# Two passes of 256 columns in place of one of 512 in every dense product of a two-block transformer kernel

## The chip, the cores and the metric

The kernel runs on one core of a Trainium2 chip. The metric is the device time of one execution in microseconds. TensorE multiplies a stationary operand of up to 128 x 128 values, which a weight load brings in, with a moving operand that streams through it column by column, and adds the products up in a PSUM bank of 128 x 512 fp32 values.

## The reference, cut to what matters

Two transformer blocks run one after the other on 512 tokens of width 1024. The first has two layers, each with two attentions (one over indexed keys, one latent), a gated merge, an output projection and an FFN with a convolution over the tokens. The second has one layer, with dilated, compressed, selected and windowed attention and a SiLU FFN. The change touches only products with weight matrices, of which these stand for all:

```python
z = h @ w_in[l]
x = x + merged @ w_out[l]
u = causal_dwconv(h @ w_up[l], conv_w[l], conv_b[l])
x = x + (jax.nn.silu(gat) * val) @ w_down[l]
```

## The kernel before, in words

Activations are kept transposed, features on the 128 partitions and the 512 tokens along the free dimension. So a product with a weight matrix is made of tiles of 128 output features by 512 tokens, a full PSUM bank each, into which the products with the 128 x 128 blocks of one column of the weight matrix are added.

To reach fp32 accuracy with the fast fp32r form, each operand is held as an upper and a lower part. The helper `matmul` (L509) makes one block product of three passes: lower weights by upper activations, upper by lower, upper by upper. Each pass is one call of `pe.matmul`, which becomes a weight load of the stationary operand and a matmul. `linear`, `linear_pair`, `linear_tiles` and `token_major` are loops over block products; in `token_major` the activations are stationary and the weights move.

Weights are streamed. SyncE brings tiles of eight blocks into `weight_ring` (four slots), GpSimd splits each tile into `w_hi` (L1948) and `w_lo` (L1954), two slots each, and TensorE waits on `weights_split` at the first block of each tile. The first pass that uses a tile signals `weights_begun`, and GpSimd then may overwrite the slot of the tile before it. The last pass of an output tile signals `tile_done`; VectorE or ScalarE then empties the bank and signals `taken`, and the bank is used again four tiles later.

Each engine runs its own list of instructions in the order in which the code is written. The two layers of the first block are a hardware loop on TensorE (L704), and so is the main part of each half of an FFN: L879 in the first block (two halves a layer, so it runs four times) and L1042 in the second (twice). Each of these six runs makes five rounds of four tiles; a round has 4 x 8 block products, 96 passes.

Some passes are not 512 columns wide: the index queries (`tokens=slice(P, S)`, 384), the second block's values (width 280), the hidden layer of the compressor (`hidden`, 256, made of operands in the arena alone) and three small products of 64.

Of the kernel before, what the change touches and what calls it, by code (L numbers as in the profile page):

```python
# [23 lines left out]
S = 512  # L24
# [65 lines left out]
                 out=64, up=352, down=176)  # L90
# [178 lines left out]
def two_blocks_kernel(nc, x_t, stream, w1, w2, par1, par2, consts, rows32, rows8, tables, spread, out_t, rows, scratch):  # L269
    with ExitStack() as ctx:  # L270
# [3 lines left out]
        def sem(name):  # L274
            return ctx.enter_context(nc.semaphore(name))
# [25 lines left out]
        def chunks(first, n):  # L301
            return arena[:, first:first + n, :]
# [39 lines left out]
        ksl, kw, v2 = chunks(47, 2), chunks(49, 2), chunks(51, 2)  # L342
# [24 lines left out]
        weights_begun = sem("weights_begun")  # L367
# [78 lines left out]
        def prob(n, width):  # L446

            n %= PROBS
            return work[:, n, 0:width] if n < 6 else sq[:, n - 6, 0:width]

        def block_bank(n):

            return (turn + stat)[n]
# [52 lines left out]
        def _(pe):  # L506
            state = {"block": 0, "begin": False}

            def matmul(out, lhs, rhs, start, stop, **kw):  # L509


                for n, (l, r) in enumerate(((lhs[1], rhs[0]), (lhs[0], rhs[1]), (lhs[0], rhs[0]))):
                    ins = pe.matmul(out, l, r, start=start and n == 0, stop=stop and n == 2, **kw)  # L513
                    if state["begin"]:
                        ins.then_inc(weights_begun, 1)
                        state["begin"] = False
                return ins

            def stage(sec, L, tiles, base):
# [179 lines left out]
            for bank, to, rows_n, table, at, width in bias_parts:  # L699
                pe.matmul(bank[0:rows_n, to:to + width], tab[:, table:table + rows_n], onehot[:, at:at + width],  # L700
                          start=True, stop=True).then_inc(rows_done, 1)


            with pe.Fori(0, LAYERS) as L:  # L704
# [20 lines left out]
                for n, key in enumerate(BESIDE_INDEX):  # L725
# [5 lines left out]
                    for q in index_batch(n):  # L731
                        b, h = INDEX[q]
                        r = slice(h % 2 * HD, h % 2 * HD + HD)
# [8 lines left out]
                for key, lhs in ((("krr",), ident), (("krp",), perm)):  # L742
                    ps = bank(key)
                    plain(pe)
                    for i in range(4):
                        ins = pe.matmul(ps[32 * i:32 * i + 32, :], lhs[32:64, 32:64], misc[32:64, 0, :], start=True,
                                        stop=True)
# [123 lines left out]
                for part, (first, n) in enumerate(HALVES):  # L871
                    n0 = A.tile_no(("up", 2 * first))
                    v0, at = A.release[n0][1], state["block"]
# [5 lines left out]
                    with pe.Fori(1 - part, n // 2) as i:  # L879
                        for s in (0, 2):  # L880

                            for k in range(DC):
                                for e in range(2):
                                    if k == 0:
                                        pe.wait_ge(A.taken["v"], L * A.count["v"] + i * 4 + (v0 + s + e - 4))
                                    w = weight(i, 4)
                                    ins = matmul(psum[(n0 + s + e) % 4][:, :], w, h_ffn(k), start=(k == 0),
                                                 stop=(k == DC - 1))
# [75 lines left out]
            def turn_compared(b):  # L964
                def turns():
                    pe.wait_ge(cmp_masked, QB)
                    pe.wait_ge(cmp_prob, b + 1)
                    plain(pe)
                    for g in range(2):
                        ins = pe.transpose(block_bank(b)[:, g * P:(g + 1) * P], work[:, b, g * P:(g + 1) * P], ident)  # L970
                    ins.then_inc(cmp_turn, 1)
                return turns
# [61 lines left out]
            for part, (first, n) in enumerate(HALVES):  # L1034
                n0 = B.tile_no(("gate", first))
                v0, a0, at = B.release[n0 + 1][1] - 1, B.release[n0][1] - 1, state["block"]
# [5 lines left out]
                with pe.Fori(1 - part, n // 2) as i:  # L1042
                    for s in (0, 2):
# [3 lines left out]
                        for k in range(DC):  # L1047
                            for e in range(2):
                                if (k, e) == (0, 1):
                                    pe.wait_ge(B.taken["v"], i * 2 + (v0 + s // 2 - 1))  # L1050
                                w = weight(i, 4)
                                ins = matmul(psum[(n0 + s + e) % 4][:, :], w, h_ffn(k), start=(k == 0),
                                             stop=(k == DC - 1))
# [8 lines left out]
        def _(act):  # L1062
# [243 lines left out]
            def block_uppers(first):  # L1306

                for n in range(first, first + 2):
                    act.wait_ge(blocks_raw, n + 1)
                    act.activation(blocks_hi[:, :, 32 * n:32 * n + 32],  # L1310
                                   block_bank(n)[:, :].rearrange("p (k n) -> p k n", n=32), ACT.Copy).then_inc(blocks_upper, 1)
# [952 lines left out]
```

## Time and profile before

| | |
|---|---|
| median of three runs | 2345.83 us (2345.34 to 2346.99) |
| the profiled execution | 2345.93 us |
| its span, first to last instruction | 2344.1 us |
| TensorE matmul busy | 2309.0 us, 11106 matmuls |
| TensorE weight load busy | 1759.3 us, 11106 loads |
| GpSimd busy | 1571.7 us |
| VectorE busy | 1073.8 us |
| ScalarE busy | 618.5 us |
| moved by DMA | 212.65 MB |

Matmuls overlap: one is shown from its start to the end of its results, while the next has already begun. The pace is therefore read from the distance between starts, not from the mean length. Weight loads (PEld) run beside the matmuls. Engine names in the rows are PE and PEld for the two sides of TensorE, DVE for VectorE, ACT for ScalarE, POOL for GpSimd and SP for SyncE.

### The profile page before, as it was taken

The page shows a single profiled execution, that of the slowest core. Times are in us where ns is not written, and L with a number is a line of the kernel's source. Part 1 is how long each engine was busy: PE and PEld are TensorE (multiplying, and loading weights), DVE is VectorE, ACT ScalarE, POOL GpSimd, SP SyncE. Part 2 cuts the span into 40 slices and gives each one's busy share as a digit, 9 for nine tenths or more (in the row PEclk, how much of TensorE's full clock was granted, in tenths as well). Part 3 has the DMA queues.
Part 4 walks back from the last instruction along what each step waited for, and adds up shares of the span by engine and source line. Part 5 has one row for each costly group of instructions (what it writes and reads, how often), then busy time and mean ns, then how long its engine had stood idle before and what let it go on. Part 6 is the DMA issues. An engine that isn't in the chain of part 4 may idle for free. (4 is left out here: it accounts for less than half of the span.)

```text
span 2344.1 us, 34637 instructions
## 1 busy us (share of the span) xinstructions
PE 2309.0 (99%) x11106; PEld 1759.3 (75%) x11106; DVE 1073.8 (46%) x2156; ACT 618.5 (26%) x1355; POOL 1571.7 (67%) x818
## 2 busy tenths in 40 slices
PE   7999999999999999999999999999999999999997
PEld 5666688878888876666888788888787667888886
DVE  5776643364314346776534643143545854110112
ACT  4334710231001233347202311012322863000001
POOL 6564377777777775643677777777766437777775
PEclk9999999999999999999999999999999999999999
DMA  6223023223233232220232232323372002323322
GB/s 208 72 78 103 11 81 99 90 90 96 92 95 94 91 99 65 80 99 20 73 98 92 89 98 90 98 90 96 131 225 90 29 19 90 91 98 91 98 90 90
DMA packets 61586, 212.65 MB, mean 91 GB/s; under 512 B 6344, under 2 KB 6728, under 8 KB 61328
## 3 DMA queue, kind: packets, MB, share of 16 engines
q1 hardware_dynamic: 54368, 194.38, 26.6%
q10 hardware_dynamic: 7088, 16.58, 2.1%
q8 instruction: 76, 1.25, 0.2%
q14 instruction: 54, 0.44, 0.1%
HBM read 208.78 MB, written 10.01 MB: 93 GB/s over the span
## 5 line engine op out<-in xcount | busy, mean ns | idle before, releaser
L513 PE MATMUL out_tile<-arena_r,w_hi 128*128 128x512 f32 (+1 forms) x5240 | 1641.1, 394 | 0.0
L513 PEld LDWEIGHTS out_tile<-arena_r,w_hi 128*128 128x128 f32 x5240 | 984.7, 188 | 232.1 <-issue 1.9
L513 PE MATMUL out_tile<-arena_r,w_lo 128*128 128x512 f32 (+1 forms) x2620 | 1042.2, 398 | 9.3 <-POOL w_lo L1954 6.5
L1948 POOL TENSOR_TENSOR w_hi<-weight_ring,cst 128x1024 fp32r<-128x1024 f32 (+1 forms) x348 | 656.3, 1886 | 536.0 <-PE out_tile L513 473.1
L1954 POOL TENSOR_TENSOR w_lo<-weight_ring,w_hi 128x1024 fp32r<-128x1024 f32 (+1 forms) x348 | 835.7, 2402 | 26.9
L513 PEld LDWEIGHTS out_tile<-arena_r,w_lo 128*128 128x128 f32 x2620 | 492.8, 188 | 152.4 <-issue 26.4
L1469 DVE TENSOR_TENSOR x<-out_tile,x 128x512 f32<-128x512 f32 x72 | 49.8, 691 | 360.4 <-PE out_tile L513 360.3
L1287 ACT ACTIVATE work<-out_tile,p 128x512 f32<-128x512 f32 x88 | 65.8, 773 | 412.1 <-PE out_tile L513 412.1
L1734 DVE SCALAR_TENSOR_TENSOR work<-out_tile,p,work 128x511 f32<-128x511 f32 x88 | 65.6, 745 | 224.6 <-ACT work L1287 224.6
L1973 POOL TENSOR_SCALAR work<-work,small 128x128 f32<-128x128 f32 (+2 forms) x60 | 34.8, 580 | 114.0 <-DVE small L1522 106.7
L1152 ACT ACTIVATE arena<-turned 128x128 f32<-128x128 f32 (+1 forms) x224 | 84.8, 430 | 47.2 <-PE turned L662 46.3
L1159 ACT ACTIVATE work<-work,small 128x128 f32<-128x128 f32 (+1 forms) x168 | 83.7, 503 | 49.8 <-DVE small L1514 49.8
L513 PE MATMUL out_tile<-w_hi,arena_r 128*128 128x512 f32 (+1 forms) x288 | 88.7, 379 | 0.0
L1381 ACT ACTIVATE work<-out_tile 128x512 f32<-128x512 f32 x22 | 13.2, 598 | 281.4 <-PE out_tile L513 281.4
L679 PE MATMUL stat<-arena 128*64 128x128 f32 x1120 | 85.7, 283 | 0.0
L1085 ACT ACTIVATE arena_r<-x,p 128x512 fp32r<-128x512 f32 x48 | 34.6, 720 | 184.0 <-DVE x L1469 184.0
L1514 DVE CUSTOM_DVE_ANT_0 work<-out_tile,arena 128x128 f32<-128x128 f32 (+1 forms) x168 | 64.7, 419 | 30.5 <-PE out_tile L837 13.7
L1269 ACT ACTIVATE work<-out_tile,p 128x512 f32<-128x512 f32 x32 | 22.0, 689 | 210.7 <-PE out_tile L513 210.7
L679 PEld LDWEIGHTS stat<-arena 128*64 128x64 f32 x1120 | 58.8, 136 | 21.4 <-issue 20.8
L513 PEld LDWEIGHTS out_tile<-w_hi,arena_r 128*128 128x128 f32 x288 | 52.3, 188 | 16.7 <-issue 6.9
L1705 DVE TENSOR_TENSOR work<-out_tile,work 128x512 f32<-128x512 f32 x14 | 9.7, 693 | 110.2 <-PE out_tile L513 110.2
L662 PEld LDWEIGHTS turned<-cst,work 128*128 128x128 f32 x336 | 36.2, 140 | 27.5 <-issue 13.8
(223 smaller groups left out, 1912.8 us busy)
## 6 DMA issues: line engine op xcount, KB each, us to landing
weight_ring<-stream SPq DMA_DIRECT2D x356, 512.0 KB, 3.5
arena<-bias_rows ACTq DMA_DIRECT2D x4, 2048.0 KB, 11.7
bias_rows<-bias_kept ACTq DMA_DIRECT2D x2, 2556.0 KB, 24.2
bias_rows<-bias_kept SPq DMA_DIRECT2D x1, 2556.0 KB, 14.9
x<-x_t SPq DMA_DIRECT2D x4, 512.0 KB, 8.7
arena<-w ACTq DMA_DIRECT2D x1, 2048.0 KB, 8.8
out_t<-arena SPq DMA_DIRECT2D x8, 256.0 KB, 2.2
cst<-consts SPq DMA_DIRECT2D x1, 576.0 KB, 14.0
```

The costliest lines, as they stand in the source:

```text
L513: ins = pe.matmul(out, l, r, start=start and n == 0, stop=stop and n == 2, **kw)
L662: ins = pe.transpose(turn[n % 2][0:width, k * P:(k + 1) * P], prob(n, k * P + width)[:, k * P:k * P + width], ident)
L679: ins = pe.matmul(stat[group % 2][e * HD:(e + 1) * HD, b * P:(b + 1) * P], values(pair[e], k), turned[0:width, 2 * (m % SLOTS) + e, k * P: ...
L1152: act.activation(turned[:, m % (2 * SLOTS), 0:w], turn[m % 2][:, 0:w], ACT.Copy)\
L1159: act.activation(prob(n, w), prob(n, w), ACT.Exp, scale=-1.0, bias=negmax[:, n % 8:n % 8 + 1], accum_out=rsum[:, n % 8:n % 8 + 1])\
L1287: act.activation(work[:, s, :], psum[(n0 + s) % 4][:, :], ACT.Identity, scale=p1[:, bass.ds(c + 2, 1)], bias=p1[:, bass.ds(c + 3, 1)])\
L1469: took(dve.tensor_tensor(x[:, j, :], tile(sec, L, key(j))[:, :], x[:, j, :], ALU.add), sec)
L1514: took(dve.tensor_tensor_reduce(prob(n, w), ps[:, 0:w], masks, 1.0, 3e38, ALU.add, ALU.min, negmax[:, c:c + 1]), sec)
L1734: dve.scalar_tensor_tensor(out=work[:, s, 1:S], in0=ps[:, 0:S - 1], scalar=p1[:, bass.ds(c + 1, 1)], in1=work[:, s, 1:S], op0=ALU.mult, op ...
L1948: pool.tensor_tensor(blocks_of(w_hi[:, s % SPLIT, :], used), blocks_of(ring[:, s, :], used), cols(cst, C_ONE).unsqueeze(1).to_broadcast([P ...
L1954: pool.tensor_tensor(blocks_of(w_lo[:, s % SPLIT, :], used), blocks_of(ring[:, s, :], used), blocks_of(w_hi[:, s % SPLIT, :].bitcast(F32), ...
L1973: pool.tensor_scalar(part, part, rinv[:, n % 8:n % 8 + 1], 1.0 if gate is None else gate, ALU.mult, ALU.mult).then_inc(sec.prob_even, 1)
```

## The change

Where the output of a block product is 512 columns wide, each of its three passes is issued as two, over the tokens (or output columns) 0 to 255 and 256 to 511, into the two halves of the same bank. Each half has its own weight load of the same stationary operand. The start flag is set on the first half of the first pass alone, and the first half signals `weights_begun`; the stop flag of the last pass is on both halves, and `tile_done` is signalled by the second.

```diff
--- before.py
+++ after.py
@@ -448,6 +448,8 @@
             n %= PROBS
             return work[:, n, 0:width] if n < 6 else sq[:, n - 6, 0:width]
 
+        token_halves = (slice(0, S // 2), slice(S // 2, S))
+
         def block_bank(n):
 
             return (turn + stat)[n]
@@ -509,11 +511,15 @@
             def matmul(out, lhs, rhs, start, stop, **kw):
 
 
+                halves = token_halves if out.shape[-1] == S else (slice(0, out.shape[-1]),)
+                if len(halves) > 1:
+                    kw["skip_group_check"] = True
                 for n, (l, r) in enumerate(((lhs[1], rhs[0]), (lhs[0], rhs[1]), (lhs[0], rhs[0]))):
-                    ins = pe.matmul(out, l, r, start=start and n == 0, stop=stop and n == 2, **kw)
-                    if state["begin"]:
-                        ins.then_inc(weights_begun, 1)
-                        state["begin"] = False
+                    for h, at in enumerate(halves):
+                        ins = pe.matmul(out[:, at], l, r[:, at], start=start and n == 0 and h == 0, stop=stop and n == 2, **kw)
+                        if state["begin"]:
+                            ins.then_inc(weights_begun, 1)
+                            state["begin"] = False
                 return ins
 
             def stage(sec, L, tiles, base):
```

TensorE's list at the head of the FFN loop L879, before the change. A row names the output and, behind the arrow, the two operands; x2 means two equal ones in a row; the register row belongs to the wait for a free bank (L885):

```order
L513 MATMUL out_tile<-arena_r,w_lo 128x512
L513 MATMUL out_tile<-arena_r,w_hi 128x512 x2
L885 REGISTER_ALU
L513 MATMUL out_tile<-arena_r,w_lo 128x512
L513 MATMUL out_tile<-arena_r,w_hi 128x512 x2
L513 MATMUL out_tile<-arena_r,w_lo 128x512
L513 MATMUL out_tile<-arena_r,w_hi 128x512 x2
```

And the same place after the change, where six more lines stand ahead in the file:

```order
L519 MATMUL out_tile<-arena_r,w_lo 128x256 x2
L519 MATMUL out_tile<-arena_r,w_hi 128x256 x4
L891 REGISTER_ALU
L519 MATMUL out_tile<-arena_r,w_lo 128x256 x2
L519 MATMUL out_tile<-arena_r,w_hi 128x256 x4
L519 MATMUL out_tile<-arena_r,w_lo 128x256 x2
L519 MATMUL out_tile<-arena_r,w_hi 128x256 x4
```

Each row of passes has become twice as many of half the width; the rows stand in the same order and nothing has moved past anything else.

## Rows read from the trace of the kernel before

**Rows 1.** The page: busy time, and the span in 40 slices.
```profile
PE 2309.0 (99%) x11106; PEld 1759.3 (75%) x11106; DVE 1073.8 (46%) x2156; ACT 618.5 (26%) x1355; POOL 1571.7 (67%) x818
...
PEclk9999999999999999999999999999999999999999
```

**Rows 2.** Groups of TensorE matmuls by form: count | busy us, mean ns.
```profile
L513 PE MATMUL out_tile<-arena_r,w_hi 128*128 128x512 f32 x5112 | 1607.5, 395 | 0.0
L513 PE MATMUL out_tile<-arena_r,w_lo 128*128 128x512 f32 x2556 | 1018.7, 399 | 4.8 <-POOL w_lo L1954 2.0 <-DVE arena_r L1496 1.1 <-DVE work L1742 1.0
L513 PE MATMUL out_tile<-w_hi,arena_r 128*128 128x512 f32 x224 | 75.9, 403 | 0.0
L513 PE MATMUL out_tile<-w_lo,arena_r 128*128 128x512 f32 x112 | 43.9, 392 | 0.0
```

**Rows 3.** Waits of TensorE: us in total, times, longest us.
```profile
PE stat L700 <- DMA cst<-consts: 10.0, 1, 10.0
PE out_tile L513 <- POOL w_lo L1954: 6.5, 8, 2.0
```

**Rows 4.** Timeline of GpSimd in an FFN stretch: start us, us.
```profile
601.27 1.89 POOL L1948 TENSOR_TENSOR w_hi<-weight_ring,cst 128x1024 fp32r<-128x1024 f32 x1 [1.23 <-PE out_tile L513]
...
606.87 1.89 POOL L1948 TENSOR_TENSOR w_hi<-weight_ring,cst 128x1024 fp32r<-128x1024 f32 x1 [1.24 <-PE out_tile L513]
```

**Rows 5.** Timeline of TensorE in the last FFN.
```profile
2240.36 0.40 PE L513 MATMUL out_tile<-arena_r,w_lo 128*128 128x512 f32 x1
...
2242.46 0.39 PE L513 MATMUL out_tile<-arena_r,w_lo 128*128 128x512 f32 x1
```

**Rows 6.** Timeline, passes of 280 columns.
```profile
1717.61 0.29 PE L513 MATMUL out_tile<-w_lo,arena_r 128*128 128x280 f32 x1
...
1719.90 0.29 PE L513 MATMUL out_tile<-w_lo,arena_r 128*128 128x280 f32 x1
```

**Rows 7.** Groups of TensorE weight loads.
```profile
L513 PEld LDWEIGHTS out_tile<-arena_r,w_hi 128*128 128x128 f32 x5240 | 984.7, 188 | 232.1 <-issue 1.9
```

**Rows 8.** Timeline and line view (ns min/median/max) of the 256-column passes.
```profile
1720.53 2.31 PE L513 MATMUL stat<-arena_r 128*128 128x256 f32 x18
1728.29 3.74 PE L513 MATMUL stat<-arena_r 128*128 128x256 f32 x30
1728.87 2.23 PEld L513 LDWEIGHTS stat<-arena_r 128*128 128x128 f32 x18
L513 PEld LDWEIGHTS stat<-arena_r x48: 187/192/192, 1720.4 to 1731.6; 128*128 128x128 f32 x48
L513 PE MATMUL stat<-arena_r x48: 274/283/283, 1720.5 to 1731.7; 128*128 128x256 f32 x48
```

**Rows 9.** Windows: us, busy PE, PEld, DVE, ACT, POOL, clock, DMA share, GB/s.
```profile
1818.00:1828.00 10.00, 10.00 (x98) 6.57 (x96) 8.57 (x33) 8.55 (x28) 5.38 (x5) 1.00 0.11 27
1728.40:1731.70 3.30, 3.30 (x30) 3.30 (x29) 0.69 (x1) 0.00 (x0) 0.00 (x0) 1.00 1.01 329
2200.00:2260.00 60.00, 60.00 (x259) 48.35 (x258) 10.41 (x15) 2.99 (x5) 45.53 (x23) 1.00 0.30 96
935.00:950.00 15.00, 15.00 (x66) 8.58 (x65) 11.53 (x19) 6.30 (x12) 6.68 (x4) 0.89 0.23 72
```

**Rows 10.** The page: instruction queue of TensorE; packets, MB.
```profile
q8 instruction: 76, 1.25, 0.2%
```

**Rows 11.** DMA in the windows 480 to 512, 512 to 600, 838.5 to 838.65.
```profile
q8 instruction: 2, 0.03, 0.4%
...
q1 hardware_dynamic: 2293, 8.34, 30.9%
...
q8 instruction: 1, 0.02, 58.0%
```

**Rows 12.** Timeline of TensorE over the layer loop's jump.
```profile
841.02 0.63 PE L513 MATMUL out_tile<-arena_r,w_hi 128*128 128x512 f32 x2
841.66 0.44 PE L513 MATMUL out_tile<-arena_r,w_lo 128*128 128x384 f32 x1
```

## The prediction

> **What bounds the kernel now.** I read the page first. TensorE is busy for 2309.0 of 2344.1 us, 99%, and the granted clock is at its upper level, 2.4 GHz, nearly throughout [rows 1]. A busy matmul engine need not be at its peak, since the bars of neighbouring matmuls overlap: a dense pass of 512 columns is shown as 392 to 403 ns long [rows 2], but starts well before the last one has ended. So the second view is the list of its waits: 10.0 us for the constants at the start, then 6.5 us in eight waits for split weights, and all others are shorter [rows 3]. There is nothing under which a slower TensorE could hide: what a pass takes longer, the kernel takes longer. GpSimd, which prepares the weights, starts a tile each 5.60 us and idles 1.23 or 1.24 us of them for TensorE [rows 4]; it has slack.
>
> The third view is the timeline, for the true pace. In a dense stretch the w_lo pass of one block product starts at 2240.36 and that of the third after it at 2242.46 [rows 5]: nine passes in 2.10 us, 0.2333 us a pass, or 0.456 ns a column. Passes of 280 columns take 2.29 us for six block products, 18 passes (1717.61 to 1719.90) [rows 6], 0.1272 us, 0.454 ns a column. So down to 280 columns the time is proportional to the columns, with no part per pass, and the weight load of each pass is fully hidden behind the pass before.
>
> **The change part by part.** It touches the dense passes whose output is 512 columns wide: 5112 + 2556 + 224 + 112 into the output tiles [rows 2], and 24 (eight block products) of the keys that `last_keys` computes, 8028. The 192 of 384 columns, 96 of 280, 48 of 256 and 9 of 64 keep their form, and so do the fp32 products of the attention.
>
> *Columns:* none are added or taken away; 2 x 256 is 512.
>
> *Weight loads:* 8028 more, of 128 columns. One load shows as 0.188 us [rows 7], which is longer than a pass of 256 columns would be at the proportional pace (0.456 x 256 = 0.1167 us), so it must overlap its own neighbours to stay hidden. Whether it does, the trace shows at one place: the compressor's 48 passes of 256 columns, each with its own 128 x 128 load, the form that the change makes of everything. There 18 loads from the inside of the run of 30 take 2.23 us from the first start to the last end; less the 0.192 us of one, 17 spacings are 2.038 us, 0.1199 us each. The two whole runs of matmuls give (2.31 - 0.283)/17 and (3.74 - 0.283)/29, both 0.1192 us [rows 8]. In the window of that stretch the load engine is busy for all of 3.30 us, where it is busy for 48.35 of 60 in a dense stretch of 512 columns [rows 9]. So at 256 columns the load is no longer free: some 3 ns of each pass stick out. For the pace of the changed kernel I take 0.1199 us, that of the inside of a run, since nearly all its passes stand in long runs. Two of them are 0.2398 us in place of 0.2333: 6.5 ns more. Times 8028 that is **+52 us**. With 0.1192, which holds the quick first passes of a run, it is 5.1 ns and +41 us. The lower bound is zero, at the proportional 0.1167; a gain is excluded because no row, at 280 or 512 columns, holds a cost per pass that a shorter pass could shed. The upper bound, for want of a nearer row, is the pace of the 280-column passes, 0.1272: 21 ns more, +169 us; the 256-column row is the same operation, so I stay near it.
>
> The Trainium skill (TensorE: Matmul & The Clock Gate, "Wait — 56ns, not 53.3ns?") gives a warm matmul N/2.4 GHz and about 2.5 ns fixed, which hides the load entirely. By that two halves would cost one more fixed part, 2.5 ns, and the change +20 us. The rows differ from it at both widths (0.2333 and 0.1199 us against 215.8 and 109.2 ns), and the sum follows the rows.
>
> *Instructions:* TensorE has twice as many dense ones to take in. It must sustain a load and a matmul in each 0.1199 us. In the attention it starts 98 matmuls in 10.00 us [rows 9], 0.102 us each, with semaphore waits among them, so the supply is fast enough. Nothing is charged.
>
> *Instruction fetches:* 76 transfers of the instruction queue feed TensorE [rows 10]; they will be some 60 more of 16 KB, nothing beside 212 MB. What can cost is a jump. At the layer loop's jump back, a fetch runs at 838.5 to 838.65 us [rows 11]; TensorE goes on from what it had taken in until the pass at about 841.26 (the second of the row at 841.02), and the next starts at 841.66: 0.40 instead of 0.233 us, 0.17 us lost [rows 12]. From about 838.6 it lived on some 11.4 queued passes; the weight load there comes 3.05 us after the fetch. With half the columns 11.4 passes last 1.4 us, so 1.6 us stick out. This jump is taken once: **+1.4 us**.
>
> *Waits:* the first half signals weights_begun, and with the same columns per product the tile's time grows from 5.6 to 5.76 us, which gives GpSimd more slack; part of the 6.5 us of waits for it shrinks. **-1 us**; bounds 0 and -6.5.
>
> *Semaphores, banks, order:* the last pass of a tile carries tile_done as before; the same four banks are used in the same order. Nothing.
>
> **Sum:** 52 + 1.4 - 1 = +52 us. The profiled execution took 2345.93 us, 1.8 more than its span and 0.1 from the median, 2345.83, so the sum goes onto the median: **2398 us**, +2.2%.
>
> **The rivals.**
> *The halves run at the proportional pace, no change.* The extra 3 ns could belong to the one stretch in which they were seen: there both operands lie in the arena, one accumulator region is hit by every pass, and the DMA engines are full (share 1.01, 329 GB/s [rows 9]). In the dense stages the weights lie in w_hi and w_lo, the halves alternate, and the share is 0.30. Against it: the 280-column passes ran beside the same traffic at the proportional pace, and all of a 256-column run shows the load engine full. It decides if the load's own pace is below 0.1167 us. Then 2 x 0.1167 is 0.2333: 2346 us. Chance 0.12, which holds the small chance of a hair faster. If only some of the passes run at 0.1167, the time lies between, 2355 to 2380: 0.09. The fixed part of the page named above, +20 us, would be 2366 and fall into this case.
>
> *The FFN loops no longer stay resident.* The six inner FFN loops take their jump back four times each, 24 in all. Today none fetches: from 512 to 600 us the weights' queue is the only one with packets, while 480 to 512 has two fetches [rows 11]. One fetch holds about (22212 - 24 x 192)/76 = 232 of the matmuls and loads [rows 1, 10]; a loop's body is 96 passes and 96 loads, 0.8 of a fetch, and becomes 384, 1.7 fetches, so that it can lie over three blocks. If the engine keeps too few, each jump fetches as the layer's does: 24 x 1.6 = 38 us more, 2436 us; uncovered, 24 x 3.05 = 73, 2471 us. For it: the layer's jump shows what a miss is. Against: the present loops are held with a block border inside almost surely and no fetch at all. Chance 0.12. The Trainium skill (Runtime: NRT & Kernel Launch, "Instruction fetch mechanics") says both that TensorE holds 128 KiB in 16 KiB blocks, by which the bigger body fits, and that the window is two blocks, by which it would not; no row here decides between them.
>
> *The clock falls.* Between 935 and 950 us the granted clock averages 0.89 [rows 9], although the engine was busy throughout. If fewer columns per microsecond made this common, each such dip would cost under 2 us; it takes ten to matter. Chance 0.03, 2420 us.
>
> **How the numbers follow.** Main case 0.64 (2384 to 2408, from +41 us less waits to +6.5 ns a pass with a rough fetch); no change 0.12; between 0.09; loops 0.12; clock 0.03. The range 2362 to 2440 leaves out the no-change case, a part of the mix and the upper half of the loop case, some 0.2. A change of 0.2% (4.7 us) is about what a measurement here tells from none: faster by more 0.02, within it 0.09, slower 0.89.
>
> **What would show it.** In the profile after: 256-column passes by the thousand, whose starts in a dense stretch lie 0.120 us apart, twelve in 1.44 us; the load engine near 100% busy in the FFN, with loads of about 0.192 us; GpSimd's idle time per tile near 1.4 us; waits of TensorE no longer than now; granted clock at 1.00; no instruction fetch inside the loops. Right on the time but wrong on the step would be a pace of 0.1167 with gaps of 1.6 us at each jump. Wrong altogether: a pace under 0.118 or over 0.122, or idle time of TensorE put down to issue.

## The result, and the profile after

The change made the kernel a little faster, and the times wider apart. The median went from 2346.54 us (22 runs, 2345.29 to 2349.98) to 2332.38 us (22 runs, 2317.03 to 2354.22). The ratio is 0.9939, 95% interval 0.9924 to 0.9954: 0.6% faster, where 2.2% slower was forecast. The ratio leaves out the slowest of the 22, which lies more than 1.5% above the fastest, though its granted clock (0.996) is that of the others. The changed kernel spreads over 37 us, that of before over 5.

The page of the profiled execution of the changed kernel (its span is 2331.8 us, its own time 2333.62 us); these are its lines on busy time, the granted clock and the queue of instruction fetches:

```profile
PE 2293.4 (98%) x19134; PEld 2119.8 (91%) x19134; DVE 1068.9 (46%) x2156; ACT 618.7 (27%) x1355; POOL 1573.6 (67%) x818
PEclk9999999999999999999999999999999999999999
q8 instruction: 121, 1.98, 0.4%
```

The dense passes in the list of groups with each shape apart:

```profile
L519 PE MATMUL out_tile<-arena_r,w_hi 128*128 128x256 f32 x10224 | 1598.6, 279 | 0.0
L519 PE MATMUL out_tile<-arena_r,w_lo 128*128 128x256 f32 x5112 | 1016.9, 280 | 4.9 <-POOL w_lo L1960 2.6 <-DVE work L1748 1.0 <-DVE arena_r L1502 0.5
```

The longest waits of TensorE behind that for the constants (line, what it waited for, us in total, times, longest):

```profile
PE out_tile L519 <- POOL w_lo L1960: 7.5, 9, 2.0
PE out_tile L519 <- DVE arena_r L1466: 2.5, 1, 2.5
```

TensorE does twice the number of dense instructions and is still the bound, as in [rows 1]; no long wait is new beside [rows 3] but one of 2.5 us, at the layer loop's jump. The load engine is shown as 91% busy. So the difference lies in the pace, and the timeline shows it. The fence holds TensorE in two stages and at the layer loop's jump, and GpSimd between:

```profile
379.86 0.40 PE L519 MATMUL out_tile<-arena_r,w_lo 128*128 128x256 f32 x2
...
380.57 0.40 PE L519 MATMUL out_tile<-arena_r,w_lo 128*128 128x256 f32 x2
...
559.96 0.39 PE L519 MATMUL out_tile<-arena_r,w_lo 128*128 128x256 f32 x2
...
560.64 0.39 PE L519 MATMUL out_tile<-arena_r,w_lo 128*128 128x256 f32 x2
...
574.01 1.90 POOL L1954 TENSOR_TENSOR w_hi<-weight_ring,cst 128x1024 fp32r<-128x1024 f32 x1 [1.07 <-PE out_tile L519]
579.46 1.89 POOL L1954 TENSOR_TENSOR w_hi<-weight_ring,cst 128x1024 fp32r<-128x1024 f32 x1 [1.06 <-PE out_tile L519]
...
834.22 0.62 PE L519 MATMUL out_tile<-arena_r,w_hi 128*128 128x256 f32 x4
837.33 0.44 PE L519 MATMUL out_tile<-arena_r,w_lo 128*128 128x384 f32 x1 [2.49 <-DVE arena_r L1466]
```

A block product (three passes of 512 columns before, six of 256 now) takes 0.71 us at 380 and 0.68 us at 560 us; before it took 0.700 everywhere [rows 5]. So there are two paces, one below and one above the old one. The windows give them better, with the passes of 100 us in the brackets behind PE's busy time (columns: window, its length, PE, its weight loads, DVE, ACT, POOL, granted clock, DMA share, GB/s):

```profile
340.00:440.00 100.00, 100.00 (x851) 100.00 (x851) 39.81 (x32) 8.67 (x14) 77.56 (x36) 1.00 0.30 95
550.00:650.00 100.00, 100.00 (x885) 100.00 (x884) 34.17 (x54) 12.14 (x18) 78.45 (x37) 1.00 0.30 95
1150.00:1250.00 100.00, 100.00 (x851) 100.00 (x850) 37.10 (x30) 8.18 (x12) 78.43 (x36) 1.00 0.30 96
1450.00:1550.00 100.00, 100.00 (x884) 100.00 (x884) 27.52 (x43) 9.54 (x14) 79.19 (x37) 1.00 0.30 95
2050.00:2150.00 100.00, 100.00 (x851) 100.00 (x851) 11.79 (x17) 1.79 (x3) 75.61 (x36) 1.00 0.30 94
```

885 passes in 100 us are 0.1130 us each, 851 are 0.1175. A window also counts the passes that cross its two borders; by the starts of block products in the timeline the two are 0.1133 us (0.680 us a product) and 0.1178 us (0.7067 us). I call them the quick and the slow rhythm. Clock, DMA share and traffic are the same in both. Every window has one or the other, held for hundreds of passes, and nothing between.

### The profile page after: what moved, and what is told of

It reads as the page before. It is cut to its first block and busy times, and to the rows that moved or that the text cites. A ratio compares the mean times of both kernels' runs of the same rounds, so it can differ in the third digit from the quotient of the medians.

```text
span 2331.8 us, 50693 instructions
## 1 busy us (share of the span) xinstructions
PE 2293.4 (98%) x19134; PEld 2119.8 (91%) x19134; DVE 1068.9 (46%) x2156; ACT 618.7 (27%) x1355; POOL 1573.6 (67%) x818
## 5 line engine op out<-in xcount | busy, mean ns | idle before, releaser
L519 PE MATMUL out_tile<-arena_r,w_hi 128*128 128x256 f32 (+1 forms) x10352 | 1632.8, 280 | 0.0
L519 PEld LDWEIGHTS out_tile<-arena_r,w_hi 128*128 128x128 f32 x10352 | 1391.6, 189 | 0.5 <-issue 0.5
L519 PE MATMUL out_tile<-arena_r,w_lo 128*128 128x256 f32 (+1 forms) x5176 | 1040.9, 282 | 12.2 <-POOL w_lo L1960 7.5
L519 PEld LDWEIGHTS out_tile<-arena_r,w_lo 128*128 128x128 f32 x5176 | 790.9, 189 | 40.7 <-issue 29.1
L519 PE MATMUL out_tile<-w_hi,arena_r 128*128 128x256 f32 (+1 forms) x512 | 89.6, 286 | 0.0
L519 PEld LDWEIGHTS out_tile<-w_hi,arena_r 128*128 128x128 f32 x512 | 72.2, 188 | 8.0 <-issue 6.9
```

Of the source, the lines that this page charges most:

```text
L519: ins = pe.matmul(out[:, at], l, r[:, at], start=start and n == 0 and h == 0, stop=stop and n == 2, **kw)
```

## The experiments

Each kernel is the changed one with the edit shown. Without an interval a time is that of one execution.

**The changed kernel again, twice.** Does the place in the program set the rhythm, or the execution?

> The changed kernel, not altered, run again. Its first profile shows two paces of the 256-column passes: 0.1133 us (layer FFNs and output products, 532 passes in 60 us) and 0.1178 us (gates and projections, last FFN, 512 passes in 60 us). Theory of the place: the pace belongs to the stage, by its operands and the traffic beside it; then every stage shows its pace again, within 2 passes per 60 us, and the span is within 3 us of 2331.8. Theory of the lock: a run of passes falls into one of two paces by how it begins and keeps it; then at least one long stage shows the other pace in this or the next run, and the span moves with it by 4.4 ns for each pass of that stage (about 13 us for the last FFN).

> The same kernel once more, unaltered. Theory of the place: the same paces in the same stages, span within 3 us of 2331.8. Theory of the lock: stages differ from the first profile or from the run before this one; the spans spread by more than 5 us.

Measured: 2339.12 and 2331.93 us. The same five windows, of the first:

```profile
340.00:440.00 100.00, 100.00 (x851) 100.00 (x850) 39.98 (x32) 8.82 (x14) 77.59 (x36) 1.00 0.30 96
550.00:650.00 100.00, 100.00 (x852) 100.00 (x851) 34.61 (x55) 12.15 (x18) 75.87 (x36) 1.00 0.28 90
1150.00:1250.00 100.00, 100.00 (x885) 100.00 (x884) 38.75 (x30) 8.83 (x13) 82.17 (x38) 1.00 0.31 101
...
2050.00:2150.00 100.00, 100.00 (x885) 100.00 (x884) 14.56 (x21) 2.99 (x5) 78.24 (x38) 1.00 0.29 96
```

and of the second:

```profile
340.00:440.00 100.00, 100.00 (x885) 100.00 (x884) 41.32 (x34) 12.38 (x19) 82.21 (x38) 1.00 0.30 98
550.00:650.00 100.00, 100.00 (x852) 100.00 (x851) 30.86 (x48) 10.71 (x16) 75.56 (x37) 1.00 0.29 95
```

The window at 340 is slow in the first two executions and quick in the third; the one at 550 is quick in the first and slow in the other two. One program, the same stages, another rhythm: it is set in each execution anew, and then holds.

By steps of 0.0200 us down or 0.0067 up for each of 2676 block products (8028 / 3), all quick is 54 us less and all slow 18 us more; the 22 runs lie within these two ends.

These rhythms account for the spread. In the timelines, 8222 passes of the first profile of the changed kernel begin a row of six at the quick pace and 7027 a row of six at the slow one; in the second profile 6723 and 8555, in the third 8119 and 7130. Priced by a sixth of these steps for each pass, the second should be 6.7 us longer than the first and the third 0.5 us longer; their spans are 5.5 us longer and 1.7 us shorter (the third lacks a fall of the clock that cost the first 1.6 us; see the part on the clock). Two kernels with the same passes that follow below, one in another order and one with added waits, have 11198 and 4028, and 5245 and 9980: priced 13 us shorter and 13 longer than the first profile, measured 11.9 shorter and 12.9 longer.

**A small disturbance.** An fp32 transpose into a spare bank ahead of each pair of output tiles in the last FFN's loops.

```
+                        pe.transpose(turn[1][:, 0:P], ident, ident)
```

> The changed kernel with one fp32 transpose of 128 columns, of constants into a bank that is idle then, ahead of each pair of output tiles in the loops of the last FFN (20 of them). It costs some 0.2 us each time, 4 us in all. Theory of the lock: each transpose ends a run of passes, so the pace of the last FFN is drawn anew each 11 us: stretches of 0.1133 appear in it, between stretches of 0.1178, or all of it goes to one of them. Theory of the place: the last FFN stays at 0.1178 throughout and the span is 4 us longer, 2336.

Measured: 2323.96 us. The last FFN now holds both rhythms, changing from one pair of tiles to the next: 1982 to 1991 us has 82 passes, 1993 to 2002 has 79, where the three executions of the changed kernel each kept one rhythm through it. Of the 20 pairs, each opened by its transpose, 7 go by the quick rhythm and 13 by the slow one; each keeps its own to the end, and from one pair to the next it changes eight times. So a foreign matmul can throw the row over, either way. The total says little here, since the stages before the last FFN drew their rhythms anew as well.

**The load's own pace.** The layers' FFN as 384 + 128 and 320 + 192 columns, the last FFN as 4 x 128 and uncut.

```
+                    state["widths"] = ((384, 128), (320, 192))[part]
+                state["widths"] = ((128, 128, 128, 128), (512,))[part]
```

> The changed kernel with other cuts of the 512 columns by stage: 384 + 128 in the first half of the FFNs of the layers, 320 + 192 in their second half, 4 x 128 in the first half of the last FFN, 512 uncut in its second half. If a load and a pass go side by side and the longer sets the pace, with the load at about 0.112 us (the nine passes of 64 columns), then a 128-column pass takes 0.112, a block product of three passes 3 x (0.175 + 0.112) = 0.86 us in the first stage, 3 x (0.146 + 0.112) = 0.77 in the second and 12 x 0.112 = 1.34 in the third, and the uncut stage 0.70; span about 2331.8 + 98 + 40 + 188 = 2660 us. If the load costs nothing of its own and only columns count, all stages take 0.68 to 0.70 us a block product and the span stays within 15 us of 2331.8.

Measured: 2652.33 us. One window for each pattern, in that order:

```profile
600.00:660.00 60.00, 60.00 (x421) 60.00 (x420) 18.64 (x29) 6.71 (x10) 36.61 (x18) 1.00 0.25 79
800.00:860.00 60.00, 60.00 (x467) 60.00 (x466) 22.39 (x35) 11.19 (x18) 42.54 (x20) 1.00 0.28 87
2100.00:2160.00 60.00, 60.00 (x540) 60.00 (x539) 13.64 (x20) 4.07 (x7) 23.33 (x12) 1.00 0.16 51
2500.00:2560.00 60.00, 60.00 (x259) 48.46 (x258) 11.81 (x17) 3.59 (x6) 45.75 (x22) 1.00 0.31 94
```

Passes of 128 columns take 60/540 = 0.111 us (0.1117 from the timeline) although their columns are half of 256. The times are those expected of a load that sets the pace (0.86, 0.77 and 1.34 us a block product). In the timeline the loads of this stage begin 50 to 55 ns behind the start of the pass before, where they begin 1 to 5 ns behind it with 256 or 512 columns throughout: here one load is held back by another, and there it is not. So 0.1117 us is the pace at which loads of 128 columns follow each other. It lies under the proportional 0.1167, so a load need not make a 256-column pass longer. The uneven pairs take 0.287 (0.1433 x 2) and 0.258 us, the uncut pass 0.2333: short passes below the load's pace are dear.

**Nearly even cuts.** 264 + 248 and 272 + 240 in the layers' FFN, 288 + 224 and 256 + 256 in the last.

```
+                    state["widths"] = ((264, 248), (272, 240))[part]
+                state["widths"] = ((288, 224), (256, 256))[part]
```

> The changed kernel with uneven halves by stage: 264 + 248 in the first half of the FFNs of the layers, 272 + 240 in their second, 288 + 224 in the first half of the last FFN, 256 + 256 in its second. Theory of the load: at 0.113 us a pass is set by the back-to-back loads (0.112 us), so a part under 256 columns gains nothing and one over it costs its columns: by the proportional pace 0.120 + 0.112 = 0.232 (first), 0.124 + 0.112 = 0.236 (second), 0.131 + 0.112 = 0.243 us (third) for two parts, against 0.227 or 0.236 at 256 + 256; only the even cut can be under 0.2333. Theory of the columns: the stall that a short pass sheds depends on its own width, and two parts of uneven width share it: all cuts down to 240 take 0.227 to 0.236 and show two paces each.

Measured: 2359.2 us; pairs of 0.2371, 0.2378 and 0.2467 us, and 0.2267 (the quick rhythm) for the even cut. Only the even cut is under 0.2333, as the first of the two theories said. Neither set of numbers was met, and I have no rule for these three; of the cuts tried, the even one alone gains, so it is not short passes as such.

**Another order.** All three passes of the first half, then those of the second.

```
+                for h, at in enumerate(halves):
+                    for n, (l, r) in enumerate(passes):
```

> The changed kernel with the order of the six passes of a block product turned: the three of the first half, then the three of the second, so that only the two upper passes load the same block in a row. If the lower pace needs the same block to be loaded twice in a row, or the two halves of one row to follow each other, every stage goes to another pace (117.8 ns or more throughout, span at least 2350). If it belongs to the width alone and to how the run begins, long stages again show 0.1133 or 0.1178 us and nothing else, and the span lies within 2305 to 2355.

Measured: 2321.67 us, with the same two rhythms (885, 884, 885, 885 and 852 passes in the five windows). Of six neighbouring pairs of passes, four load the same block twice in the changed kernel and two in this one; the halves of one pass no longer follow each other. So neither of the two is needed for the rhythms. Whether they need any such pair at all was not tried.

**One pass of three cut.** Only the w_lo pass of each block product is cut; the other two stay at 512.

```
-                    for h, at in enumerate(halves):
+                    for h, at in enumerate(halves if n == 0 else (slice(0, out.shape[-1]),)):
```

> One part of the change alone: the first of the three passes of a block product (lower weights) is cut into halves, the two others stay at 512 columns. 2676 cut passes in place of 8028. If each cut pass sheds its own share of the gain, a block product takes 0.4667 + 0.227 = 0.693 us at the quick pace or 0.4667 + 0.2356 = 0.702 at the slow one, and the span lies between 2344 - 18 and 2344 + 7. If the gain needs an unbroken row of short passes, since it is the loads one behind the other that set the pace, all stages take 0.700 us a block product, as before, and the span is within 3 us of 2344.

> The kernel with only the first pass of each block product cut, timed against the kernel before. If its one pace of 0.6933 us a block product belongs to the form, all its executions lie within 3 us of 2331, a ratio of 0.9935 (0.993 to 0.994). If it too has a second pace that one profile missed, its executions spread over more than 10 us, as those of the changed kernel did (2317 to 2354).

Measured: 2331.09 us, and in the timed comparison 2330.58 us (5 runs, 2330.08 to 2332.68), ratio 0.9936, interval 0.9923 to 0.995. The timeline:

```profile
599.75 0.39 PE L519 MATMUL out_tile<-arena_r,w_lo 128*128 128x256 f32 x2
599.98 0.62 PE L519 MATMUL out_tile<-arena_r,w_hi 128*128 128x512 f32 x2
600.44 0.40 PE L519 MATMUL out_tile<-arena_r,w_lo 128*128 128x256 f32 x2
```

A block product takes 0.693 us in every stage, and the spread is 2.6 us, not 37. The same gain as by cutting everything, with a third of the extra instructions, and steady. A long row of short passes is not needed for it.

**TensorE waits for its own last tile** at the start of five stages, so that each begins with an empty pipe.

```
+                        A.wait_done(pe, L, ("up", 3))
+                        plain(pe)
```

> The changed kernel with TensorE made to wait for its own last tile at five places, ahead of the gates of each layer, of the FFN loop of each layer and of the last FFN's loop, so that it stops for some 0.3 us and the long run begins after a true stop. In the three profiles 12 of 13 runs that began after a gap of about 0.52 us, a stop, went to 0.1133 us. If the start of a run decides and a stop leads to the quick pace, all five long stages (1548, 2970, 1548, 2970 and 3000 passes) show 885 passes in 100 us, and the span is that of the first profile less 4.45 ns x (1554 + 1554 + 3018) = 27 us, plus 2 for the stops: 2307. If a stop leads to no pace in particular, some of the five show 851, and the span stays in 2315 to 2355.

Measured: 2346.54 us; four of the five windows are slow (851, 885, 851, 852, 851). A stop does not lead to the quick rhythm. This theory fell.

**Which pass is cut.** By stage: the third alone; the first two; the last two; the first and third; the second alone.

```
+                state["cut"] = (2,)
+                    state["cut"] = ((0, 1), (1, 2))[part]
+                state["cut"] = ((0, 2), (1,))[part]
```

> Which passes of a block product are cut, by stage: gates and projections the third alone, first half of the layers' FFNs the first two, their second half the last two, first half of the last FFN the first and third, its second half the second alone, all else the first alone. Measured so far: no cut 0.700 us a block product, the first alone 0.6933 in every stage, all three 0.680 or 0.7067. Theory of the share: each cut pass among uncut ones sheds 6.7 ns, so one cut gives 0.6933 (578 passes in 100 us) whichever it is, two give 0.6867 (728 passes in 100 us), and every stage has one pace; the span is about 2344 - 6.7 ns x (2676 + 1152 + 864) = 2313. Theory of the row: what brings the two paces is a long row of cut passes without an uncut one; with any uncut pass in the product the pace is one and steady, but two cuts need not give twice one. Theory of the weights: only the pass with the lower weights sheds, as its load comes from the other tile; then gates and projections and the second half of the last FFN stay at 0.700 (571 passes in 100 us).

Measured: 2350.21 us. Windows with the third alone, the first two, the last two, and the first and third:

```profile
340.00:440.00 100.00, 100.00 (x579) 87.70 (x578) 40.93 (x33) 10.23 (x16) 79.93 (x37) 1.00 0.30 95
550.00:650.00 100.00, 100.00 (x710) 93.41 (x708) 33.22 (x52) 12.16 (x18) 75.67 (x36) 1.00 0.30 95
1450.00:1550.00 100.00, 100.00 (x709) 93.40 (x708) 20.61 (x33) 7.47 (x11) 75.50 (x36) 1.00 0.30 95
2050.00:2150.00 100.00, 100.00 (x709) 93.41 (x708) 13.88 (x20) 3.00 (x5) 76.96 (x36) 1.00 0.29 94
```

One cut is 0.6933 us a product whichever pass it is (four passes, 579 in 100 us; the second alone, at 2220 to 2250 us, has the same by its starts); two cuts are 0.7067 whichever two (five passes, 709): more cuts, and slower than none. No theory that adds up a price per cut pass can hold. What counts is the pattern of short and long.

**Patterns.** By stage, over successive block products: one cut and none in turn; seven with all cut and then one with none; all and one; all and none; one and two.

```
+                pattern = state.get("cut", ((0,),))
+                cut = pattern[state.get("product", 0) % len(pattern)]
```

> Patterns over block products, by stage (all: three passes cut; one: the first cut; two: the first two; none). Gates and projections: one, none in turn. First half of the layers' FFNs: seven times all, then none. Second half: all, one in turn. First half of the last FFN: all, none in turn. Second half: one, two in turn. All else: one. Measured so far per block product: none 0.7000, one 0.6933, two 0.7067, all 0.6800 or 0.7067 us. If the pace is a sum over products, the means are 0.6967, then 0.6825 or 0.7058, then 0.6867 or 0.7000, then 0.6900 or 0.7033, then 0.7000 us. If it is a matter of the repeating pattern as a whole, as two cuts costing more than one or none suggest, the means are others, each still a whole number of steps of 6.67 ns over its period; and a single uncut product in eight makes the layers' first FFN half one pace in both layers.

Measured: 2334.67 us; means of 0.700, 0.6937, 0.6867, 0.695 and 0.6967 us a product. A sum of the paces of the single products would have been 0.6967, 0.6825 or 0.7058, 0.6867 or 0.7000, 0.6900 or 0.7033, and 0.7000: it holds for the third alone. The second pattern shows what happens at each uncut product:

```profile
600.65 0.64 PE L522 MATMUL out_tile<-arena_r,w_hi 128*128 128x256 f32 x4
601.12 0.39 PE L522 MATMUL out_tile<-arena_r,w_lo 128*128 128x512 f32 x1
601.35 0.63 PE L522 MATMUL out_tile<-arena_r,w_hi 128*128 128x512 f32 x2
601.82 0.39 PE L522 MATMUL out_tile<-arena_r,w_lo 128*128 128x256 f32 x2
602.05 0.62 PE L522 MATMUL out_tile<-arena_r,w_hi 128*128 128x256 f32 x4
602.50 0.39 PE L522 MATMUL out_tile<-arena_r,w_lo 128*128 128x256 f32 x2
...
606.58 0.39 PE L522 MATMUL out_tile<-arena_r,w_lo 128*128 128x512 f32 x1
606.81 0.63 PE L522 MATMUL out_tile<-arena_r,w_hi 128*128 128x512 f32 x2
...
607.51 0.64 PE L522 MATMUL out_tile<-arena_r,w_hi 128*128 128x256 f32 x4
607.98 0.40 PE L522 MATMUL out_tile<-arena_r,w_lo 128*128 128x256 f32 x2
```

Ahead of 601.12 four passes of w_hi take 0.47 us; behind the three long ones they take 0.45 (602.05 to 602.50); at 606.58 three long ones come again, and it is 0.47 again (607.51 to 607.98). Three long passes in a row flip the rhythm: wherever such a row stands in this run with at least five short passes of one rhythm on either side and no stop, the rhythm changes, in 211 of 212 cases. In the stage "all and one" two long passes stand between short ones, and what follows them is always quick (238 cases, in all but two of which it was quick before as well). That suggested the next three.

**Two long passes in every eighth block product,** and in every second.

```
+                state["product"] = state.get("product", 0) + 1
+                short = state["product"] % 8 > 0
-                    for h, at in enumerate(halves):
+                    for h, at in enumerate(halves if n == 0 or short else (slice(0, out.shape[-1]),)):
```

> The changed kernel, but in every eighth block product only the first pass is cut: 44 short passes, then two long ones. Theory of the pattern, from the runs so far: two long passes between short ones always end in the quick rhythm (0.226, 0.236, 0.118, then 0.1133 each), from whichever rhythm they come, so every long stage goes at (7 x 0.680 + 0.6933)/8 = 0.6817 us a block product in every execution; span 2344 - 18.3 ns x 2676 = 2295, plus 2 to 5 for jumps and starts: 2297 to 2300 us, and the executions lie within 5 us of each other. Theory of chance: the rhythm is drawn again at each long pass; then the stages show a mixture, the median is near 2330 and the spread over 10 us.

> The same with every second block product: eight short passes, two long. By the pattern: 0.6867 us a block product in every stage, as the one stage that had this form showed in both layers, span 2344 - 13.3 ns x 2676 = 2308, plus 0 to 5, executions within 5 us of each other. By chance: near 2330 with a spread over 10 us.

Measured: every eighth 2304.44 us (5 runs, 2303.81 to 2307.81), ratio 0.9825, interval 0.9811 to 0.9838; every second 2315.07 us (4 runs, 2314.76 to 2316.92), ratio 0.987, interval 0.9855 to 0.9885. Of the first, a stretch of eight products in the timeline:

```profile
600.23 0.39 PE L521 MATMUL out_tile<-arena_r,w_lo 128*128 128x256 f32 x2
...
600.91 0.39 PE L521 MATMUL out_tile<-arena_r,w_lo 128*128 128x256 f32 x2
601.14 0.62 PE L521 MATMUL out_tile<-arena_r,w_hi 128*128 128x512 f32 x2
601.60 0.39 PE L521 MATMUL out_tile<-arena_r,w_lo 128*128 128x256 f32 x2
...
605.69 0.39 PE L521 MATMUL out_tile<-arena_r,w_lo 128*128 128x256 f32 x2
```

and two windows:

```profile
550.00:650.00 100.00, 100.00 (x847) 98.47 (x846) 31.55 (x49) 10.72 (x16) 79.05 (x38) 1.00 0.29 98
2050.00:2150.00 100.00, 100.00 (x845) 98.46 (x845) 13.07 (x19) 1.97 (x4) 78.61 (x37) 1.00 0.30 98
```

From 600.23 to 605.69 us are eight products, 0.6825 us each, with the mixed one (600.91 to 601.60) at 0.69; the 845 to 847 passes of the windows, 46 in eight products, say 0.680; by the starts over whole stages it is 0.6817, just (7 x 0.680 + 0.6933)/8 as expected. Every second product gives 0.6867, also as expected. So the quick rhythm holds in every window, and the narrow times suggest in every execution. The mixed product costs 0.0133 us more than the others. The median, 2304.44 us, is 4 us above the 2297 to 2300 expected: the spans of the two profiles differ by 39.9 us, where 49 less 2 to 5 was expected. Some of the short rows among the attention go by the slow rhythm.

The timelines also correct the theory. Counted where no stop lies near, two long passes keep a quick row quick in 288 of 293 cases (every second product: 1188 of 1198), but a slow row is quick behind them in 8 of 16 only (24 of 47). So a pair mainly holds the quick rhythm; a slow row may pass several pairs before it turns. The whole difference between this kernel and the changed one is one product in eight with four passes in place of six.

**One long pass in every eighth product,** the counterpart.

```
+                    for h, at in enumerate(halves if n < 2 or short else (slice(0, out.shape[-1]),)):
```

> As the first kernel of this call, but in every eighth block product the first two passes are cut and the third alone is long: 46 short passes, one long. Theory of the pattern: one long pass always ends in the slow rhythm (0.236, then 0.118 each), so every long stage goes at 0.7067 us a block product and the span is 2344 + 6.7 ns x 2676 = 2362 us. If any long pass at all is what leads to the quick rhythm, it is 0.681 us a block product, 2297 us; if long passes do nothing, stages show 0.680 and 0.7067 as those of the changed kernel, 2317 to 2355.

Measured: 2361.67 us. All five windows have 833 or 834 passes, 47 of them to eight products: 0.705 us each by the window and 0.7067 by the starts, the slow rhythm everywhere, as expected. The one long pass is followed by the slow rhythm in 279 of 284 cases behind a slow row (one is neither) and in 27 of 27 behind a quick one. So the gap of 57 us between this kernel and that with two long passes in every eighth product hangs on one pass in 24 being cut or not.

## Why the prediction was wrong

**What bounds the kernel** was right: TensorE's pace is the kernel's time, and nothing else moved.

**Weight loads, the step that failed.** It forecast 0.1199 us a pass and +52 us, from "at 256 columns the load is no longer free", and excluded a gain "because no row, at 280 or 512 columns, holds a cost per pass that a shorter pass could shed". Measured were 0.1133 and 0.1178 us. In the profiled execution, matched one by one with the kernel before, 1361 block products are quicker by about 0.0200 us and 1165 slower by about 0.0067, which is 1361 x (-0.0200) + 1165 x 0.0067 = -19.4 us in place of +52. The sign of being wrong altogether that the prediction named, a pace under 0.118, is what both rhythms show. It gave "faster by more" a chance of 0.02. Two things in it were wrong. First, the price was read at one place, the 48 passes of the compressor [rows 8]. It was no artefact, as that place is as slow in the changed kernel, where its run of 30 looks so in the timeline:

```profile
1714.13 3.76 PE L519 MATMUL stat<-arena_r 128*128 128x256 f32 x30
```

But the same operation has other paces elsewhere, and what makes this place different the runs don't tell. Second, I took "proportional from 280 to 512 columns" for "no part per pass". A row that can show only one width at a time can't exclude a gain: 0.2333 us for 512 columns was not what the engine can do with them, and two halves do it in 0.2267. The load engine full to 100% was read as a load that sticks out; it is as full at 128 columns, where a pass takes 0.1117 us. In the run of the compressor too the loads begin 2 to 5 ns behind the start of the pass before, so nothing shows that the load makes up its 0.120 us. Full means only that loads are shown one behind the other; their own pace was not reached with 256 columns. The formula that the prediction cites from the Trainium skill (TensorE: Matmul & The Clock Gate, "Wait — 56ns, not 53.3ns?") has no term for a load; that it "hides the load entirely" was my reading of it. Its price for the change, +20 us, missed the sign as well.

**Instructions** were free, as said. **Instruction fetches:** the loops stayed resident. At the prediction's 232 a fetch, and without the four repeated turns of each loop, the added passes and loads make (8028 - 24 x 96) x 2 / 232 = 49 more transfers, not its 60; 76 + 49 = 125 stand against the 121 made. In all six loops there is a stretch of some 100 us without any (such as 516.8 to 619.3 us, 1335.9 to 1438.5 and 2162.0 to 2267.0). So that rival fell. Of the two statements that the prediction cites from the Trainium skill (Runtime: NRT & Kernel Launch, "Instruction fetch mechanics"), this agrees with the 128 KiB; the window of two blocks could hold a body of 1.7 fetches only where it happens to lie within two, which no run here looked at.

**The layer's jump** had the right sign and was a little undersized. The starts lie 834.56 (the fourth of the row at 834.22) and 837.33 apart, 2.77 us, of which a pass would take 0.12: 2.65 lost, against 0.17 before [rows 12] and 1.6 forecast. The view names VectorE's work, done at 836.58, as what TensorE waited for, but the run with two long passes in every eighth product shows that it is not needed there:

```profile
826.10 0.62 PE L521 MATMUL out_tile<-arena_r,w_hi 128*128 128x256 f32 x4
827.76 0.69 DVE L1468 TENSOR_TENSOR arena_r<-turned,arena_r 128x512 fp32r<-128x512 f32 x1 [0.32 <-issue]
828.17 0.44 PE L521 MATMUL out_tile<-arena_r,w_lo 128*128 128x384 f32 x1 [1.45 <-issue]
```

The same instruction of VectorE, 1.3 us behind the last start in both runs, ends at 828.45 here, and TensorE has gone on before, at 828.17. What both runs share is a fetch, at 834.54 and at 825.51; TensorE goes on 2.8 and 2.7 us after it. In the second run it came 0.9 us before the last start (826.44), and 1.6 us are lost, the size forecast. In the changed kernel it came 0.02 us before, so that next to nothing was left to live on, where the prediction had 11.4 queued passes; that is the other 1 us. Why the fetch came later there the runs don't tell.

**Waits:** -1 us was forecast, since a slower TensorE gives GpSimd slack; they went from 6.5 to 7.5. The reason fell with the sign of the pace. GpSimd starts a tile each 5.44 us in the quick stage and idles 1.06 of it, not 1.24 [rows 4] and not the 1.4 forecast.

**Sum:** -19.4 + 2.5 (jump) + 1.6 (the fall of the clock, below) + 0.7 = -14.6 us, where the spans differ by 2344.1 - 2331.8 = 12.3. The 0.7 us lie at the start, where passes of 384 columns are 0.32 us apart until 20.7 us, in the kernel before until 19.4 us, and 0.175 later on. The other 2.3 us are many small steps, the 1.0 us of waits among them.

**The clock** was at its upper level, 2.4 GHz, nearly throughout, but not all the time. In this execution it fell to the lower one, 1.2 GHz, at the head of the dense row that begins at 116.23 us, behind sixteen fp32 products over 32 partitions; TensorE had been busy without a break since 114.00. In the kernel before the same row begins at 116.52 and keeps the upper level. The windows, first after and then before:

```profile
116.20:119.90 3.70, 3.70 (x22) 3.67 (x19) 3.30 (x6) 1.20 (x2) 3.02 (x2) 0.54 0.03 7
```

```profile
116.90:120.00 3.10, 3.10 (x15) 2.51 (x14) 2.70 (x6) 1.49 (x3) 2.73 (x2) 1.00 0.02 5
```

Passes of 256 columns are 0.213 us apart there, and three block products take 1.6 us more than before. The second profile of the changed kernel has 0.54 in this window too, the third has 1.00, so the change does not always bring it. This is the *clock* rival (chance 0.03) in kind, and its price of under 2 us for each fall was right; it took ten to matter, and here was one more than before.

The rival *halves at the proportional pace* had the nearest time, 2346, but by accident: it is a mean of a quicker and a slower rhythm, and no stage ran at it.

**What stays open.** What inside TensorE makes the rhythms; what picks one at the start of a row; why two long passes keep the quick one, one leads to the slow one, and three flip it; the paces of the nearly even cuts. The experiments show that the pattern of long and short passes sets the pace; they show no cause within the engine.

## What to carry to other kernels

When TensorE is the bound, take its pace from the starts in the timeline for each form and pattern of passes, never from one width or one stretch: here the same 256-column pass cost 0.1133, 0.1178 or 0.120 us. A wide spread between executions of one kernel is worth a look at windows by stage, since it may be two steady states of the engine; a periodic small irregularity (here, two uncut passes in every eighth block product) can hold the better one, and it took 1.75% off a kernel whose TensorE was 99% busy. Try such patterns by measurement, also those that "should" be neutral, since the price of a mix is not the sum of its parts.

## What the hardware showed

- A pass of 512 columns with its own load takes 0.2333 us, at a granted clock of the upper level, 2.4 GHz. Two of 256 take 0.2267 at best.
- With cuts at 256 columns the block-product paces are 0.680, 0.6933, 0.700 and 0.7067 us, each a multiple of 0.0067 us from the next. One cut pass of three gives the second whichever it is, two the fourth, none the third, and three the first or the fourth.
- With all passes short, both ends are self-sustaining over thousands of passes. Two long passes keep the quick one (288 of 293 cases) and end the slow one in about half of the cases (8 of 16, 24 of 47); one leads to the slow one (306 of 311), and three swap them (211 of 212).
- At the lower clock, where the window shows 0.54, passes of 256 columns are 0.213 us apart, at the upper one 0.1133 or 0.1178.
- The load of 128 columns, shown as 0.188 us, follows the last one after 0.1117 us on average in the stage of 4 x 128 columns, the least seen.
